# Moving the spread of an expert's rows from the head of the round into each size's body

## What is computed

```python
def moe_swiglu(h, w_router, wg, wu, wd):
    logits = (h @ w_router).astype(jnp.float32)
    top_v, top_i = lax.top_k(logits, TOP_K)
    top_p = jax.nn.softmax(top_v, axis=-1)
    gates = jnp.sum(jax.nn.one_hot(top_i, N_EXPERTS, dtype=jnp.float32) * top_p[..., None], axis=-2)
    act = jax.nn.silu(jnp.einsum('bnd,edf->bnef', h, wg)) * jnp.einsum('bnd,edf->bnef', h, wu)
    act = act * gates.astype(h.dtype)[..., None]
    return jnp.einsum('bnef,efd->bnd', act, wd)
```

## Time and profile before

| | us |
|---|---|
| median of 3 runs | 2124.86 (2123.4 to 2126.49) |
| the profiled execution | 2122.26 |
| its span | 2120.5 |
| the expert rounds | about 1011 to 2085 |
| TensorE busy (page) | 1798.7 (85%) |
| VectorE, ScalarE busy | 607.0 (29%), 390.6 (18%) |

### The profile page before, as it was taken

The page is one execution under the profiler, slowest core; times in us unless marked ns, Lnnn a source line. Parts: engine busy times, 40 slices in busy tenths (PEclk is TensorE's granted clock), DMA queues, the critical chain, the costliest instruction groups (busy, mean ns, idle before and its releaser), DMA issues.

```text
span 2120.5 us, 22940 instructions
## 1 busy us (share of the span) xinstructions
PE 1798.7 (85%) x8823; PEld 1008.1 (48%) x8824; DVE 607.0 (29%) x1113; ACT 390.6 (18%) x780; POOL 55.6 (3%) x78
## 2 busy tenths in 40 slices
PE   4977888999986978878889995769998699999972
PEld 1753565888863844557234442323433244444321
DVE  1444564333326355554111011102001120000115
ACT  2423423222213323402010010010001010000100
POOL 1010000000000010000100000000000000000000
PEclk8987888999997977887999997769999699999997
DMA  9134414333333234240996659996645963444491
GB/s 340 60 132 159 142 65 156 131 119 119 119 134 125 100 138 154 100 167 13 347 367 238 236 190 392 393 389 244 217 154 195 390 235 121 151 149 155 131 366 51
DMA packets 198799, 401.96 MB, mean 190 GB/s; under 512 B 10872, under 2 KB 51832, under 8 KB 198688
## 3 DMA queue, kind: packets, MB, share of 16 engines
q1 hardware_dynamic: 195280, 389.06, 51.1%
q0 software_dynamic: 3408, 11.34, 1.5%
HBM read 397.48 MB, written 2.88 MB: 189 GB/s over the span
## 4 chain that ended last, share of the span: by engine, by line
PE 72%; DVE 8%; DMA 8%; SPq 4%; issue 4%; ACT 1%; POOL 1%; ACTq 0%; DVEq 0%; POOLq 0%
PE ps L1407 22%; PE ps L1707 14%; PE ps L1751 7%; PE ps L1712 4%; PE ps L1718 4%; SPq L519 3%; PE ps L1667 3%; PE ps L1364 3%; DMA qkv<-in_w_moe_up 2%; PE ps L1499 2%; DMA d_ring<-in_w_moe_up 2%; DMA gu_ring<-in_w_moe_up 2%; PE ps L1758 2%; PE ps L1764 1%; PE ps L1477 1%
## 5 line engine op out<-in xcount | busy, mean ns | idle before, releaser
L1324 DVE TENSOR_TENSOR cst<-cst,ps 128x256 f32<-128x256 f32 (+2 forms) x92 | 34.3, 373 | 827.8 <-ACT cst L849 827.8
L1407 PE MATMUL ps<-d_ring_parts,scratch_parts 128*128 128x512 f32 (+1 forms) x444 | 172.1, 388 | 7.9 <-issue 5.0
L1707 PE MATMUL ps<-gu_ring,hT 128*128 128x512 f32 x384 | 172.6, 594 | 0.0
L856 ACT ACTIVATE cst<-ps 128x256 f32<-128x256 f32 (+1 forms) x92 | 31.8, 346 | 585.3 <-PE ps L1734 585.3
L1407 PE MATMUL ps<-gu_ring_parts,scratch_parts 128*128 128x512 f32 (+1 forms) x336 | 128.9, 384 | 0.0
L1407 PE MATMUL ps<-d_ring_parts,hT_parts 128*128 128x512 f32 (+1 forms) x312 | 119.3, 382 | 0.0
L1707 PEld LDWEIGHTS ps<-gu_ring,hT 128*128 128x128 f32 x384 | 70.7, 190 | 83.9 <-issue 83.9
L1718 PE MATMUL ps<-gu_ring,hT 128*32 128x256 f32 x960 | 77.1, 466 | 35.0 <-DMA gu_ring<-in_w_moe_up 35.0
L1407 PE MATMUL ps<-gu_ring_parts,o_parts 128*128 128x512 f32 x264 | 104.3, 395 | 0.0
L1667 PE MATMUL ps<-qkv,small 128*128 128x512 f32 x144 | 76.7, 695 | 31.9 <-issue 31.9
L1407 PEld LDWEIGHTS ps<-d_ring_parts,scratch_parts 128*128 128x128 f32 x444 | 84.4, 190 | 26.9 <-issue 5.8
(11 more groups left out here) (279 smaller groups left out, 2697.9 us busy)
## 6 DMA issues: line engine op xcount, KB each, us to landing
gu_ring<-in_w_ada SPq DMA_DIRECT2D x48, 1024.0 KB, 7.6
gu_ring<-in_w_moe_gate SPq DMA_DIRECT2D x96, 512.0 KB, 8.2
gu_ring<-in_w_moe_up SPq DMA_DIRECT2D x96, 512.0 KB, 9.2
gu_ring<-in_w_moe_down SPq DMA_DIRECT2D x96, 512.0 KB, 8.7
d_ring<-in_w_moe_gate SPq DMA_DIRECT2D x48, 512.0 KB, 11.7
d_ring<-in_w_moe_up SPq DMA_DIRECT2D x48, 512.0 KB, 11.3
d_ring<-in_w_moe_down SPq DMA_DIRECT2D x48, 512.0 KB, 10.4
gu_ring<-in_w_in SPq DMA_DIRECT2D x16, 1024.0 KB, 7.4
```

Source lines behind the costliest of these rows:

```text
L1324: dve.tensor_tensor(hid_e[0:rows, k % 2, 0:f], hid_e[0:rows, k % 2, 0:f], ps[0:rows, 6 + k % 2, f:2 * f], ALU.mult).then_inc(hid_ready, 1 ...
L1407: ins = pe.matmul(out, a, w, start=(start and n == 0), stop=(stop and n == 2))
L1707: ins = pe.matmul(ps[:, bank, :].rearrange("p (a f) -> p a f", a=2), hT[:, kc, P * g:P * g + P], wt[:, :, FC * h:FC * h + FC], start=st, s ...
```

## The change

TensorE's `at_top` becomes empty. In every body, behind `gate_up_of(0, 0)` and `gate_up_of(0, 1)`, the spread of the last expert is issued if `t > 0`. Its register load, its waits and its Ifs on the number of blocks move with it, and exist nine times instead of once. VectorE, ScalarE and SyncE are as before; the last spread, behind the loop, too.

```diff
                     if k < len(steps):
                         gate_up_of(k, 1)
+                    if k == 0:
+                        with pe.If(t > 0):
+                            spread(t)
                     if k:
                         if k == 1:
                             pe.wait_ge(spread_added, t * 6 + 7)
                         down_of(k - 1)
 
             def at_top(t):
-                with pe.If(t > 0):
-                    spread(t)
+                pass
```

## The result

The changed kernel is slower by 0.6%. Its median is 2137.38 us (four runs, 2136.67 to 2139.18) against 2124.13 for the kernel before (four runs beside it, 2122.86 to 2126.49): a ratio of 1.0064, 95% interval 1.0049 to 1.0079, or +13.3 us. The profiled execution took 2139.18, with a span of 2137.4, 16.9 more than before; 2.7 of this difference arise ahead of the rounds, where the code is untouched. The work is the same: TensorE has 8823 matmul records in both.

What follows compares the result with a forecast made beforehand. TensorE was taken to bound rounds 1, 4 and 6, the weights the other rounds. Head terms of -0.8, -5.0, -5.0 and -0.5 sum to -11.3 us, giving a median of 2113.6 us, range from just below 2105 to 2127.

Steps and rivals of the forecast that it cites:

- The first new gap: Idle TensorE between the last down matmul and step 0's gate and up; taken as 2.8 us, bounds 2.2 and 3.6.
- the jump from the spread to the body costs nothing in the trace: After the spread at a head: entering the body adds no idle time, since 1091.81 + 7.10 meets 1098.75.
- The second new gap: Between step 0's matmuls and the moved spread: idle for Ifs and load, taken as 0.5 us, bounds 0 and 1.57.
- ScalarE's 2.23 and 3.17: ScalarE's idle us from last copy to first instruction in the next body, used as nearest measure for TensorE's 2.8.
- saves the slow stretch too: At heads: a gap under about 2.6 to 3 us avoids the 1.2 GHz clock, about 1.8 to 2.6 us.
- the slower rival: If chain in nine bodies stalls behind step 0, 2.75 us at six heads, plus slow clock: 2139 us, chance 0.13.
- the third gap: Between spread and step 1 in rounds with several blocks: wait for VectorE's hT copy, 2.4 us, 2.9 at head 6.
- heads 2 and 5: Heads into DMA-bound rounds: earlier weight loads gain 5.0 us each, counted to the ends of rounds 3 and 5.
- The three early granules: At heads 2, 5 and 7, three ring slots freed by step 0 let weight loads issue before the spread.
- the stream's lead from position 15: Behind head 2, weight loads run on from ring position 15, issued at 1275.1, 5.0 us ahead; head 5 likewise.
- Head 7: Head into the three-block round: no clock saving, early weight loads worth nothing, split gap partly hidden: -0.5 us.
- Heads 1, 4 and 6: Heads into TensorE-bound rounds: saved slow clock pays for the wait on VectorE; +0.3, -0.8 and -0.3, together -0.8 us.

Runs made afterwards that it cites:

- The filler: Changed kernel with six useless 128x512 matmuls between the old round and the jump to the body: 2151.04 us, ratio 1.0129.
- the reversed order: Changed kernel with TensorE's nine bodies laid down in the opposite order, no instruction added or dropped: 2147.97 us, ratio 1.0112.
- the first hybrid: Changed kernel with the spread behind step 0 only for a tail of 32 alone, other sizes at the top: 2122.08 us, ratio 0.9988.

## Why the prediction was wrong

It said 2113.6, within 2104 to 2127, with 0.69 on faster; the kernel takes 2137.4, slower where faster was forecast. Point by point:

- **The step that failed: "The first new gap ... I take 2.8; bounds 2.2 and 3.6".** It is 7.24, 3.43, 3.22, 3.85, 2.49, 8.91 and 4.24: outside the bounds at four of seven heads. The upper bound was reasoned as "today's gap, which has more in it". But today's gap ends in the spread, which stands at the loop's top; it contains no jump into a body. What stood behind the spread was left out.
- **The reading under it: "the jump from the spread to the body costs nothing in the trace".** Without hints, the gap with the jump in it (6.41 and 7.56 at heads 1 and 6) is 5.3 and 6.1 longer than the one without it (1.08 and 1.42); in the kernel before that time lay under 7.1 and 7.8 us of spread, and so did the instruction transfer. The filler shows it too: matmuls of 6.8 us put into the gap at head 6 delay step 0 by 0.7. The kernel before without hints shows it in the old order: there the spread is 5.41, shorter than the fetch, and 2.12 us stick out. The second new gap was priced from that same free jump; there it held, since step 0 covers it.
- **ScalarE's 2.23 and 3.17 were no measure for TensorE.** They are mostly that engine's own nine hints: without them the 3.17 is 0.86. TensorE's gap has its hints in it too, but at heads 1, 6 and 7 a fetch besides, which ScalarE's rows don't show.
- **The clock: "saves the slow stretch too".** It follows the gap. Step 0 takes 10.02, 8.82 and 8.72 instead of 7.03 at heads 1, 4 and 6. At head 1 the failed terms are 4.4 of gap and 3.1 of clock, together 7.5, less the 0.5 taken for the second gap: the 7.0 by which that head was missed. At heads 4 and 6 the wait for hT brings a second slow stretch, 1.9 and 1.7, which the sum did not have. The point of "under about 2.6 to 3 us" doesn't hold either: behind 2.49 at head 5 step 0 takes 5.35 instead of 3.66.
- **Right: the second gap**, 0.22 at head 3 and at most 0.1 at the others, below the 0.5 taken. The Trainium skill's queue of 64 for TensorE (TensorE: Matmul & The Clock Gate, on engine queue depths) would have given this; the trace agrees. The Trainium skill's rule on taken branches (Runtime: NRT & Kernel Launch, Instruction fetch mechanics) was weighed in the slower rival at the skip inside the body, where nothing shows behind step 0's matmuls. The runs fit it one jump earlier, at the entry of the body. The rival's 2139 is near the result by its size, not by its mechanism: it put the price between step 0 and the spread.
- **Right: the third gap**, 2.37, 2.32 and 2.94 against 2.4 and 2.9.
- **Half right: heads 2 and 5**, -4.1 against -5.0 and -7.8 against -5.0. The three early granules and the stream's lead from position 15 are there. But at head 2 step 1 comes 1.0 sooner and not 2.9, since the gap is 3.43 and step 0 slow (5.06 instead of 3.5); position 15 goes out 25.1 behind the last down matmul, where 23.6 was forecast, and by the prediction's own working that leaves a lead of 3.5. (Its 3.1 for VectorE's product is 2.9 by its own four terms, and its 6.4 from step 1 to position 15 measures 6.0.) At head 5 the stall of 7.16, which was left in place, fell to 2.49: in the kernel before an instruction transfer lands 5.37 behind the last matmul there (the one of the earlier trace rows), 1.79 ahead of the gap's end, in the changed one at 1.34. That this head gave more than forecast was luck.
- **Head 7** was given -0.5 and is +4.9: gap 4.24 instead of 2.32, and step 0 at 9.6.

Heads 1, 4 and 6 were worth -0.8 in the sum and are +19.6; that is the miss. The change does win 11.9 at heads 2 and 5, as argued, and loses 24.5 at heads 1, 4, 6 and 7. The median rose by 13.3 and not by the span's 16.9, most of the rest being the 2.7 ahead of the rounds.

**What stays open.** Why a late transfer falls into the gaps of heads 1, 6 and 7 and not of heads 2 to 5, and why it starts as late as 5.8 us behind the last matmul at head 6; the reversed order shows that place matters (head 4 from 3.85 to 8.36) but heads 1, 6 and 7 didn't follow it. And whether the 2.5 us of the nine hints is the compares or what the hints start. That the wait is a fetch of instructions is inferred from what covers it, moves it and lengthens it, and from the 1.8 to 2.0 us between a landing and the gap's end. In the other runs these are 1.7 to 2.2 at the long gaps ahead of step 0, but 3.1 at head 2 without the hint for the branch back. No row says for which engine a transfer is, or what the 1.8 us hold.

## What to carry to other kernels

A jump that costs nothing in a trace may only be covered: before moving work away from in front of it, ask what else is queued there, and give the new gap today's gap plus the length of the work moved as its upper bound (here 3.59 + 7.10 = 10.7 us at head 1 and 11.8 at head 6, not 3.6; 7.24 and 8.91 were measured). Look on the instruction queue, too, for transfers under the work that is to be moved. Around a loop with large bodies on TensorE, keep queued matmuls ahead of the jump in, and test branch hints one by one: the one given a body ahead was worth 8.5 us, the nine compared at the loop's top cost 15. And where an order pays in rounds bound by transfers and not in those bound by TensorE, it can be chosen for each size; here that gained 2 us (0.1%), and places that the edit doesn't touch, probably by the shifted code, took back most of what was forecast.

## What the runs showed of the hardware

- The way of TensorE from one large body into the next (branch back, load, nine hinted Ifs, jump), with nothing queued, left it idle for 2.5 to 8.9 us; 2.1 to 2.5 us of the long ones go when the weight stream beside it falls from about 400 to about 100 GB/s.
- The nine of these gaps that are over 4 us, in the changed and the reversed kernel, end 1.8 to 2.0 us behind the landing of a 16 KB transfer on the instruction queue. With matmuls queued, the transfers land at the same time and the matmuls run on.
- The same instructions laid down in another order moved one such wait from 3.85 to 8.36, and a hybrid of both orders made the untouched last spread end 6.2 later behind the last round.
- Nine Ifs with hints cost about 2.5 us at a loop's head on TensorE. On ScalarE they cost 2.2 and 2.3 at the two heads read, but the kernel's time doesn't change without them (2104.67 against 2104.70).
- After idle stretches of 3.2 us and more the changed kernel's step 0 began at 0.50 to 0.64 of full clock, at all six heads; in the first hybrid it ran at full clock (3.66) behind 3.30 at head 5. Shorter ones went both ways: the filler ran at 0.59 behind 2.42, step 0 of round 5 at 0.69 behind 2.49, step 1 of round 1 took its full-clock 1.93 behind 2.37, that of round 4 5.57 instead of 3.65 behind 2.32.
